# Two transformer layers with routed experts: a router with moving tokens, the shared expert split around it, sums from row halves

## The reference

```python
hx2 = modulate(rms_norm(x, g_pre_ffn), sh2x, sc2x)
x = x + g2x * rms_norm(moe(hx2), g_post_ffn)

def moe(t):
    scores = sigmoid(t @ w_router)                       # (tokens, 32)
    idx = top_k(scores + b_router, 4)
    w = scores[idx] / sum(scores[idx]) * 2.5
    routed = sum_e comb[:, e] * (silu(t @ w_gate_e[e]) * (t @ w_up_e[e])) @ w_down_e[e]
    shared = (silu(t @ w_gate_s) * (t @ w_up_s)) @ w_down_s
    return routed + shared
```

## Time and profile before

| | |
|---|---|
| median of 3 runs | 1782.97 us (1781.2 to 1783.63) |
| the profiled execution, its own time | 1783.4 us |
| its span, first to last instruction | 1781.6 us |
| TensorE busy | 1557.9 us, 87% |
| VectorE busy | 759.8 us, 43% |
| ScalarE, GpSimd busy | 458.1 us, 289.1 us |
| mean granted TensorE clock | 0.936 of full speed |

### The profile page before, as it was taken

How to read it: one execution, slowest core, us unless ns; L and a number is a source line. 1 busy time by engine, 2 the same in 40 slices (tenths; PEclk the granted TensorE clock), 3 DMA queues, 4 the chain that set the end, 5 groups by cost and what they waited for, 6 DMA issues and landing times.

```text
span 1781.6 us, 21596 instructions
## 1 busy us (share of the span) xinstructions
PE 1557.9 (87%) x7272; PEld 1026.3 (58%) x7272; DVE 759.8 (43%) x1415; ACT 458.1 (26%) x910; POOL 289.1 (16%) x526
## 2 busy tenths in 40 slices
PE   5999999999988898999999970899999789787782
PEld 3677565777766744444444430695699665444441
DVE  1577868778855322111111117353756621111113
ACT  1332234332324310111111102333455512111111
POOL 3000000001120031222222220000001033333320
PEclk8999999999999798999999995999999989999986
DMA  9642430356563412888888818412136559999993
GB/s 326 232 166 98 142 118 1 119 193 237 175 245 146 192 68 103 320 326 319 319 320 328 327 60 301 142 51 95 48 142 223 218 193 376 414 415 415 416 385 135
DMA packets 123125, 394.11 MB, mean 221 GB/s; under 512 B 16372, under 2 KB 20932, under 8 KB 104368
## 3 DMA queue, kind: packets, MB, share of 16 engines
q1 hardware_dynamic: 103264, 359.42, 54.1%
q0 software_dynamic: 18432, 30.56, 4.9%
q10 hardware_dynamic: 1360, 3.23, 0.5%
HBM read 389.88 MB, written 30.61 MB: 236 GB/s over the span
## 4 chain that ended last, share of the span: by engine, by line
PE 69%; DMA 14%; DVE 11%; issue 4%; ACT 1%; SPq 1%; POOLq 0%; POOL 0%; ACTq 0%; DVEq 0%
PE ps L1128 15%; PE ps L1424 12%; DMA ring<-in_w_up_e 10%; PE ps L1452 6%; PE ps L1309 3%; PE ps L1430 3%; PE ps L1311 3%; PE ps L1310 3%; PE ps L1280 2%; DVE Grow L1573 2%; PE ps L1208 2%; PE ps L1413 2%; PE ps L1209 2%; PE ps L1210 2%; PE ps L1319 1%
## 5 line engine op out<-in xcount | busy, mean ns | idle before, releaser
L1424 PE MATMUL ps<-ring,oT_b 128*128 128x512 f32 x512 | 225.9, 594 | 0.0
L1938 DVE TENSOR_TENSOR head<-ps,head 128x128 f32<-128x128 f32 (+1 forms) x68 | 24.1, 354 | 401.4 <-ACT head L1076 401.4
L1430 PE MATMUL ps<-ring,oT_b 128*64 128x256 f32 x1152 | 153.5, 427 | 45.0 <-DMA ring<-in_w_up_e 45.0
L1424 PEld LDWEIGHTS ps<-ring,oT_b 128*128 128x128 f32 x512 | 95.3, 191 | 107.6 <-issue 107.6
L1430 PEld LDWEIGHTS ps<-ring,oT_b 128*64 128x64 f32 x1152 | 93.4, 154 | 96.6 <-DMA ring<-in_w_up_e 36.1
L1309 PE MATMUL ps<-ring_lo,w_hi 128*128 128x512 f32 (+1 forms) x384 | 131.8, 343 | 3.9 <-DVE ring_lo L1763 3.7
L1573 DVE SCALAR_TENSOR_TENSOR Grow<-ring,small,Grow 128x512 f32<-128x512 f32 x182 | 131.1, 749 | 3.8
L1310 PE MATMUL ps<-h_lo,w_hi 128*128 128x512 f32 (+1 forms) x384 | 130.0, 339 | 0.0
L1076 ACT ACTIVATE head<-ps 128x128 f32<-128x128 f32 (+1 forms) x68 | 22.2, 327 | 397.2 <-PE ps L1424 208.7
L755 POOL TENSOR_TENSOR qkv<-qkv,head 128x512 f32<-128x512 f32 (+1 forms) x32 | 36.0, 1125 | 437.1 <-DVE head L1795 437.1
L1208 PE MATMUL ps<-ring_lo,oT_lo 128*128 128x512 f32 (+1 forms) x256 | 87.2, 341 | 5.1 <-DVE ring_lo L1620 5.0
(11 more groups left out here) (284 smaller groups left out, 3030.7 us busy)
## 6 DMA issues: line engine op xcount, KB each, us to landing
ring<-in_w_gate_e SPq DMA_DIRECT2D x68, 1024.0 KB, 8.6
ring<-in_w_up_e SPq DMA_DIRECT2D x68, 1024.0 KB, 11.4
ring<-in_w_ada SPq DMA_DIRECT2D x34, 1024.0 KB, 5.3
qkv<-in_w_down_e SPq DMA_DIRECT2D x34, 1024.0 KB, 11.3
ring<-in_w_in SPq DMA_DIRECT2D x13, 2048.0 KB, 10.4
cT<-in_w_down_e SPq DMA_DIRECT2D x17, 1024.0 KB, 11.1
fT<-in_w_down_e SPq DMA_DIRECT2D x17, 1024.0 KB, 12.9
qkv<-in_w_in SPq DMA_DIRECT2D x7, 2048.0 KB, 10.5
```

The source lines that it names most:

```text
L1424: ins = nc.tensor.matmul(ps[:, o:o + 512], x[:, tile(k)], gu[u][:, :, k, :], start=k == 0, stop=k == KC - 1)
L1430: ins = nc.tensor.matmul(ps[64 * f:64 * f + 64, o:o + 256], xk, w, start=k == 0, stop=k == KC - 1, skip_group_check=True)
```

## The change

The router's product has its operands exchanged: the router's 32 columns are stationary and all tokens of `hT` move, one product for each k, each waiting only for its own k of `hT`. ACT takes the sigmoid of the transposed scores, and TensorE transposes them back (group "score") behind the first tile's rows. The transposes before it are taken tile by tile as far as the tiles are there, the last tile's at the end. The shared gate and up products become four groups of the planner: one stands between "rank" and "turn", one between "turn" and "items", two behind "items". `make_rows` comes ahead of the second half's activation. The shared down product stands behind the last expert and stays in PSUM, a tile in two banks, where `combine` takes it as the first addend. `picked` is loaded in halves (two rows of a token), eight loads of 1 MB in layer 0, each with a buffer of its own, with no wait between them. Layer 1's first three weight loads are issued ahead of them. `add_experts` follows its own tile's `combine`, and layer 1's first norm of a tile follows the next tile's `combine`. Tiles whose sum TensorE would take (`by_product`) are none.

```diff
+        g.add("act", l, "rt")
         for t in range(act):
             for j in range(2):
                 g.add("act", l, "hrow", t, j)
+            if t == 0:
+                g.add("dve", l, "score")
+        g.add("dve", l, "rank")
+        g.add("act", l, "sgu", 0, 0)
+        g.add("dve", l, "turn")
+        g.add("dve", l, "sgu", 0, 1)
+        g.add("dve", l, "items")
+        g.add("act", l, "sgu", 1, 0)
+        g.add("dve", l, "sgu", 1, 1)
...
+        score_T = tmp2[0:NE, 1, :]
+        silu_s = act_s = tmp2
+        dn_s = hT[:, 0:4, :].rearrange("p a b -> p (a b)").rearrange("p (k n) -> p k n", k=2)
+        late_junk = oT_b[:, 0:DM]
...
+        by_sum = [(0, 1, 2, 3), (0, 1)]
+        by_product = [(), ()]
...
+        acc_of_tile = lambda t: ps[:, DM * t:DM * t + DM]
...
                     else:
-                        sp.wait_ge(sgu_full[l], 2)
+                        wait_full(sp, l, "sgu", 1, 1)
...
-                sp.wait_ge(merged[l], 2 * KC)
-                sp.dma_start(dn_s, I["w_down_s"][l].rearrange("(k p) n -> p k n", p=P)).then_inc(sdn_loaded, 16)
...
+                sp.dma_start(dn_s, I["w_down_s"][l].rearrange("(k p) n -> p k n", p=P)).then_inc(sdn_loaded, 16)
+                if l == 0:
+                    for n in range(first_item[1], first_item[1] + 3):
+                        load_item(n)
                 for u in range(UNROLL):
                     sp.wait_ge(y_stored[l][u], more * 16 + 16 * BLOCKS)
                 for t in range(act):
-                    if t >= 2:
-                        sp.wait_ge(combined[l], t - 1)
-                    sp.dma_start(picked[t % 2].rearrange("p (k d) -> p k d", k=TOPK),
-                                 y_rows[l].rearrange("(t p k) d -> t p k d", p=P, k=TOPK)[t]).then_inc(picked_loaded[t % 2][l], 16)
+                    for i in range(2):
+                        sp.dma_start(picked[t][i], y_rows[l].rearrange("(t p k) d -> t p k d", p=P, k=TOPK)[t][:, 2 * i:2 * i + 2, :])\
+                            .then_inc(picked_loaded[t][i], 16)
...
-                for t in range(act):
-                    wait_full(act_e, l, "rt", t)
-                    nc.scalar.activation(score[:, t, :], bank(l, "rt", t)[:, 0:NE], ACT.Sigmoid).then_inc(emptied["act"], 1)
+                wait_full(act_e, l, "rt")
+                nc.scalar.activation(score_T[:, 0:n_tok], bank(l, "rt")[0:NE, 0:n_tok], ACT.Sigmoid).then_inc(emptied["act"], 1)
...
+                def add_square(t):
+                    wait_combined(act_e, l, t)
+                    square_at(l, acc_of_tile(t) if t in by_product[l] else acc[:, t, :], t, DM, late_junk)
+                    root_at(l, t, t + 1)
+
+                def next_square(t):
+                    act_e.wait_ge(x_updated[l], act + t + 1)
+                    act_e.wait_ge(ssq_ready[l], all_squares[l])
+                    square_at(l + 1, xres[:, t, :], t, DM, late_junk)
+                    root_at(l + 1, t, t + 1)
+                    act_e.wait_ge(ssq_ready[l + 1], all_squares[l + 1])
+
                 for t in range(act):
-                    act_e.wait_ge(combined[l], t + 1)
-                    square(acc[:, t, :], t, DM)
-                    root(t, t + 1)
+                    add_square(t)
+                    if l == 0:
+                        next_square(t)
...
+                def transpose_late(n, tiles):
+                    dst = []
+                    for ks in (range(6), range(6, KC)):
+                        for t in range(tiles - 1):
+                            pe.wait_ge(xn_ready[l], NTILE + t + 1)
+                            for k in ks:
+                                if t == 0:
+                                    dst.append(group(l, "h", n, k))
+                                cols = xn[:, t, :].rearrange("p (q k) -> p k q", k=KC)[:, k, :]
+                                nc.tensor.transpose(dst[k][:, tile(t)], cols, ident[:, :])
+                    pe.wait_ge(xn_ready[l], NTILE + tiles)
+                    for k in range(KC):
+                        cols = xn[:, tiles - 1, :].rearrange("p (q k) -> p k q", k=KC)[:, k, :]
+                        nc.tensor.transpose(dst[k][:, tile(tiles - 1)], cols, ident[:, :]).then_inc(psum_full, 1)
...
-                for t in range(act):
-                    dst = group(l, "rt", t)
-                    chain(dst[:, 0:NE], [(hT[:, k, tile(t)], wr[:, k, :]) for k in range(KC)]).then_inc(psum_full, 1)
+                dst = group(l, "rt")
+                for k in range(KC):
+                    wait_emptied(pe, l, "h", 2, k)
+                    ins = nc.tensor.matmul(dst[0:NE, 0:n_tok], wr[:, k, :], hT[:, k, 0:n_tok], start=k == 0, stop=k == KC - 1)
+                ins.then_inc(psum_full, 1)
...
+                    if t == 0:
+                        dst = group(l, "score")
+                        wait_emptied(pe, l, "rt")
+                        for a in range(act):
+                            ins = nc.tensor.transpose(dst[:, NE * a:NE * a + NE], score_T[:, tile(a)], ident[0:NE, 0:NE])
+                        ins.then_inc(psum_full, 1)
...
+                def shared_in(f, a):
+                    dst = group(l, "sgu", f, a)
+                    pe.wait_ge(shared_loaded, 32 * (l + 1))
+                    w = gu[SLOTS - 1]
+                    chain(dst[:, 0:n_tok], [(w[:, a, k, P * f:P * f + P], hT[:, k, 0:n_tok]) for k in range(KC)]).then_inc(psum_full, 1)
...
+                shared_in(0, 0)
...
+                shared_in(0, 1)
...
+                shared_in(1, 0)
+                shared_in(1, 1)
+                wait_emptied(pe, l, "sgu", 1, 0)
+                wait_emptied(pe, l, "sgu", 1, 1)
                 more = nc.tensor.value_load(more_u[0:1, 0:1], min_val=0, max_val=4)
...
+                pe.wait_ge(sdn_loaded, 16 * (l + 1))
+                for t in by_sum[l] + by_product[l]:
+                    if t == act - 1:
+                        pe.wait_ge(y_act[l], more * UNROLL + NE)
+                        if not narrow:
+                            pe.wait_ge(y_dve[l], more * UNROLL + NE)
+                    for hf in range(2):
+                        ins = chain(acc_of_tile(t)[:, 512 * hf:512 * hf + 512],
+                                    [(act_s[:, f, tile(t)], dn_s[:, f, 512 * hf:512 * hf + 512]) for f in range(2)])
+                    if t in by_sum[l]:
+                        ins.then_inc(acc_full, 1)
...
-                wait_emptied(dve, l, "rt", act - 1)
+                wait_full(dve, l, "score")
+                scores = bank(l, "score")[:, 0:NE * act].rearrange("p (t e) -> p t e", e=NE)
...
+                V.tensor_copy(sc, scores).then_inc(emptied["dve"], 1)
...
+                activate_shared(0)
                 wait_full(dve, l, "items")
...
-                if l:
-                    make_rows()
-                for g in range(2 * act):
-                    b = 4 + g % 4
-                    dve.wait_ge(sdn_full[l], g + 1)
-                    V.tensor_copy(acc[:, g // 2, 512 * (g % 2):512 * (g % 2) + 512], ps[:, 512 * b:512 * b + 512])\
-                        .then_inc(sdn_taken[l], 1)
-                if l == 0:
-                    make_rows()
+                make_rows()
+                activate_shared(1)
+                wait_emptied(dve, l, "items")
...
                 def combine(t):
+                    wait_acc(dve, l, t)
                     for k in range(TOPK):
+                        dve.wait_ge(picked_loaded[t][k // 2], 16 * (l + 1))
+                        ins = V.scalar_tensor_tensor(acc[:, t, :], picked[t][k // 2][:, k % 2, :], pick_w[:, t, k:k + 1],
+                                                     acc[:, t, :] if k else acc_of_tile(t), ALU.mult, ALU.add)
...
+                def next_norm(t):
+                    invert_norm(t, l + 1)
+                    normalise_x(t, l + 1)
+
                 for t in range(act):
                     combine(t)
-                    if t >= 1:
-                        add_experts(t - 1)
-                add_experts(act - 1)
+                    if l == 0 and t:
+                        next_norm(t - 1)
+                    add_experts(t)
+                if l == 0:
+                    next_norm(act - 1)
```

183 lines of the change are left out of this document (84 added, 99 removed).

## The result

The changed kernel takes **1757.2 us** (median of 4 runs, 1756.19 to 1760.33) against 1782.09 us for the kernel before on the same chip (4 runs, 1780.95 to 1783.63): ratio 0.9863, 95% interval 0.9846 to 0.988. The forecast was 1757. The profiled execution took 1756.19 us, its span is 1754.1 us, and the mean granted clock is 0.945 (before 0.936).

The account below looks back on a forecast made before the run. The chain of waits was taken to lie on TensorE through layer 0's experts, with layer 1's experts bound by DMA. Terms -25.7 + 1.8 - 4.0 + 1.6 = -26.3 on 1783.4 gave 1757; range 1750 to 1765.

Parts of the forecast that it names:

- Router, layer 0: Layer 0's way from router to experts: first expert transposes at 661.6 instead of 687.3, 25.7 us gained (bounds 23 to 27.4).
- full clock: Layer 0's router product: assumed to run at full clock, 6.9 us; at low clock 12.0 to 13.7 us.
- Row numbers at 653.4: Layer 0: DVE can make row numbers at 653.4 instead of 680.76, because the copies are gone.
- the gather: Layer 0's first gather, meeting expert 3's 2 MB load: taken as 6.0 us, against 4.37 alone and median 6.9 under load.
- gathers late: Rival: first gather takes 9 us in both layers, half the router product runs at low clock; 1763; 12%.
- Experts of layer 0: Layer 0's expert loop: unchanged and TensorE-bound, so no gain.
- End of layer 0: Layer 0's sums and norms after the last expert: 1.8 us lost (bounds 0 to 4).
- halves share: Rival at layer 0's end: the eight loads advance together and end near 1087; 15 us more, 1772; 3%.
- Router, layer 1: Layer 1's way to the experts: first transposes at about 1458.5 to 1459 against 1462.97, 4.0 us gained (3 to 5).
- the DMA-bound loop carries a gain one for one: Layer 1's experts: the weight stream moves with the first expert, so the 4.0 us gained carry through.
- End of layer 1: From issue of the row loads to layer 1's last addition: 25.7 against 24.1, 1.6 us lost (0.5 to 3).
- a clock that stays low: Rival: granted clock at half through all 64 shared gate and up instructions, experts start later; 1790 us; 3%.

Follow-up runs that it names:

- gather_free: Changed kernel, with SP issuing expert 3's 2 MB of gate and up weights only after the first gather has landed, in both layers: 1753.1 us, ratio 0.9836.
- rows_first: Kernel before, with layer 0's row numbers computed ahead of the eight copies of the shared down product: 1779.5 us, ratio 0.9981.
- once more: The changed kernel run again unaltered, to measure what varies between executions: 1756.9 us.
- skewed: Changed kernel, with layer ends reordered: sums of tile t, then norm and addition of t-1, then in layer 0 the next norm of t-2: 1750.2 us, ratio 0.9824.

## Why the prediction was right, and where it was not

**Router, layer 0** (forecast 25.7, measured 23.3). VectorE's start 6.4 us sooner: relative to the output product it was 7.7. The product starts 3.4 us sooner, takes 7.03 instead of 12.53, and sigmoid and turned scores take 1.2 back; full clock was the right choice. The routing on VectorE was to grow by 0.2 us, and it grew by 1.3 up to the first table DMA (12.4 against 11.2), 1.1 of it a longer wait of VectorE for TensorE's ranks (1.83 us against 0.77). Row numbers at 653.4: 650.6, of which 2.3 is the sooner start of the whole. TensorE there before the gathered rows: yes, at 653.1. **The step that failed is the gather.** I took 6.0 us between the 4.4 alone and the 6.9 median; it took 9.0, the value of the rival "gathers late" in this layer (4.5 in layer 1), and between 6.9 and 9.0 in seven profiles, because its issue falls beside SyncE's 2 MB. gather_free shows it: with the same gather and only that load held back, 4.4. That rival's own price was added up 1 us short: 3 + 3 + 1 on 1757 is 1764, not 1763.

**Experts of layer 0** (0): 0.3 less, inside the spread of 369 to 372.

**End of layer 0** (+1.8; issue to the last transpose 55.1 before, 55.7 after, so +0.6). The first half landed 1 us sooner than worked out and the second 1 us later (5.3 and 10.3 us behind the issue, forecast 6.3 and 9.3), with VectorE idle for 2.4 between them; what repaid it was the tile, 9.7 us instead of 10.1, three times. That the halves come one by one was right, so "halves share" fell.

**Router, layer 1** (4.0 gained, and carried whole). To the experts it is 3.0 us in the recorded pair. It is not settled how much the change gives: the profile before had a quick router product there (4.90 us against 7.00 for the same instructions in rows_first) and the changed kernel's profile a slow one (4.68 against 3.64 once more). The stage takes 48.5 or 51.4 us in the kernel before and rows_first, and 42.9 to 46.2 in profiles of the changed order in which the weights are not held back, so by these profiles the gain lies between 2.3 and 8.5. **That the DMA-bound loop carries a gain one for one was not borne out by the pair**: 2.0 us were given back in it. The loop takes 289.0 to 290.7 us in all profiles of the changed order and 287.5 to 289.9 in the three of the old one, for reasons that no run here separates.

**End of layer 1** (+1.6): +1.2 from issue to the last addition. The terms of the forecast add up to 25.6, not 25.7, which changes nothing.

In the recorded pair the four places give 23.3 + 3.0 - 0.9 - 1.2 = 24.2 us, layer 1's loop takes 2.0 back, layer 0's experts add 0.3, and 5.0 lie in stages that vary by themselves: 27.5 between the spans. The medians, over four runs each, give 24.9. The rival of a clock that stays low did not come true: the three later quarters of gate and up ran at 1.00. Part of its mechanism did: the first quarter, behind a pause of 2.25 us and the narrow rank products, ran at 0.77 and took 9.2 us instead of 7.1, hidden behind the table.

What the prediction did not ask is whether the change left time lying there. Each end was priced as a small loss with the squares bare, and skewed shows that keeping the old order would have turned it into a gain.

## What to carry to other kernels

Two small transfers on the critical path lost time because a 2 MB prefetch with time to spare was issued at nearly the same moment: the gather 2.5 to 4.6 us, and in two of the variants the table read 4.2. A wait that holds the prefetch back cost nothing that a stage shows. When a sum is moved so that it feeds a norm directly, keep one tile of other work between a tile's sum and the use of its norm. Before a total is taken as proof of a sum of terms, cut both spans at shared landmarks: here 5 us of it lay in code that had not changed.

## What the runs showed of the hardware

- Layer 0's first gather of 128 rows (512 KB) took 4.4 us alone and 6.9 to 9.0 us when 2 MB were issued beside it on SyncE's queue; layer 1's table read took 3.65 us or 7.9. The Trainium skill (DMA: Bandwidth & Descriptors, Queues, rings and completion order) says that each DMA engine takes turns between its queues, packet by packet. The traces agree for a part of the gather's delay. In the changed kernel SyncE's queue moved 112 packets from 654.2 to 657.1 us and GpSimd's queue none; from 657.1 to 661.4 both moved, 168 and 376. GpSimd's first packet started 4.4 us behind the issue of the gather, against 1.7 in gather_free, so 2.7 of the 4.6 us lost lie ahead of it, and the rest where the two queues move side by side. In the changed kernel once more the first packet started 1.7 us behind the issue, ahead of the weights, and all 2.5 us lost lie in the shared stretch. Over the seven profiles, GpSimd's first packet came 1.7 us behind the issue where the weights' first packet came 2.2 behind it, 3.0 where it came 1.7 behind, and 4.2 to 4.6 where it came 0.9 to 1.5 behind. So it seems to matter whose packets come first; why the gather then waits is not shown.
- How late they get depends on a small difference in issue: the read took 7.9 us with the weights 0.8 us behind it, 3.65 with them 2.2 us behind. Layer 0's gather took 9.0 us with the weights 0.3 us behind it, 8.3 to 8.8 at 0.5, 7.6 at 0.7 and 6.9 at 0.8; with them 0.1 us ahead it took 8.4, and 3.4 us ahead 5.3. Layer 1's first gather took 3.4 us alone, and with the weights ahead by 2.7, 2.9, 3.2, 3.8 and 4.1 us it took 5.6, 5.0, 4.6, 4.5 and 4.2.
- In layer 0, with 128 tokens stationary and 32 columns moving, 64 matmuls ran at half clock for 13.8 us; with the router's 32 columns stationary and 512 tokens moving, 16 ran at full clock for 7.0 us. In layer 1, 32 of the narrow ones took 7.00 us at a clock of 0.50, 4.90 at 0.74 and 4.09 at 0.90, so narrow matmuls do not always run at half clock.
- The same work differs between executions by 3.5 us in each of two long stretches (591.8 to 595.3 and 300.0 to 303.5 us).
